# New call orders for the four compute engines ahead of the channel-pair loop, without the identity transposes

## What is computed

```python
h = rmsnorm(x, norm_mix_g)
a_val, a_gate, b_in = split(h @ w_in, [512, 1024])          # 1024 x 1536
u  = a_val * sigmoid(a_gate)
ya = silu(layernorm(causal_dwconv31(u) + conv_a_b))         # 31 taps, 512 channels
yb = (window_mean(b_in, w = 2, 4, 8, 16) - b_in) @ pool_w * pool_scale
x  = x + concat(ya, yb) @ w_out
h  = rmsnorm(x, norm_ffn_g)
gate, val = split(h @ w_up, 2)                              # 1024 x 5632
x  = x + (silu(causal_dwconv3(gate) + conv_f_b) * val) @ w_down
return rmsnorm(x, norm_final_g)
```

## Time and profile before

| | |
|---|---|
| median of 3 runs | 921.43 us (921.29 to 921.58) |
| profiled execution: its own time, first to last instruction | 918.0 us |
| TensorE busy | 897.2 us (98%) |
| VectorE busy | 690.0 us (75%) |
| GpSimd busy | 664.8 us (72%) |
| ScalarE busy | 412.6 us (45%) |
| `idle_turns` | 82 matmuls, 9.8 us busy |

### The profile page before, as it was taken

One profiled execution on the slowest core, in us unless ns is written; L12 is line 12 of the kernel. 1 busy time (PEld: TensorE's weight loads), 2 busy tenths in 40 slices (PEclk: granted clock), 3 DMA queues, 4 the chain that ended last, 5 costly groups with the idle time before them and its releaser, 6 DMA issues.

```text
span 918.0 us, 11316 instructions
## 1 busy us (share of the span) xinstructions
PE 897.2 (98%) x4088; PEld 742.8 (81%) x4088; DVE 690.0 (75%) x731; ACT 412.6 (45%) x626; POOL 664.8 (72%) x501
## 2 busy tenths in 40 slices
PE   6999999999999999999999999999999999999996
PEld 5888888888887788788888888888888888888875
DVE  6898998996787565686867768587685876858667
ACT  7566655863654422433424334243342433424335
POOL 4399998483289754977959779597795977959821
PEclk9999999999999999999999999999999999999998
DMA  8321011151001121021120211302113021121114
GB/s 286 98 73 65 1 46 47 47 161 46 0 12 35 59 79 46 12 81 46 46 92 12 84 44 46 92 12 91 35 47 92 21 83 36 46 92 29 40 47 184
DMA packets 62775, 57.74 MB, mean 63 GB/s; under 512 B 2137, under 2 KB 55897, under 8 KB 62716
## 3 DMA queue, kind: packets, MB, share of 16 engines
q1 hardware_dynamic: 62720, 57.01, 19.7%
HBM read 52.81 MB, written 4.19 MB: 62 GB/s over the span
## 4 chain that ended last, share of the span: by engine, by line
PE 82%; DVE 5%; ACT 4%; POOL 4%; issue 4%; DMA 0%; DVEq 0%; SPq 0%; POOLq 0%; ACTq 0%
PE slot L2295 81%; POOL conv L689 3%; PE slot L2331 1%; ACT prod L1072 1%; DVE act_lo L1616 1%; DVE x_sb L1938 1%; POOL tmp L675 1%; DVE tmp L1603 0%; DMA x_sb<-in_x 0%; ACT junk L959 0%; ACT act_hi L968 0%; DVE sums L1804 0%; ACT slot L1101 0%; DVE bn L1706 0%; DVE x_sb L1734 0%
## 5 line engine op out<-in xcount | busy, mean ns | idle before, releaser
L734 POOL TENSOR_TENSOR ring<-raw,ring 128x512 fp32r<-128x512 f32 x199 | 272.6, 1390 | 117.1 <-ACT ring L1148 116.9
L1148 ACT ACTIVATE ring<-raw 128x512 fp32r<-128x512 f32 x203 | 121.0, 625 | 249.1 <-POOL raw L757 117.0
L2295 PE MATMUL slot<-act_hi,ring 128*128 128x512 f32 x680 | 219.7, 390 | 1.2 <-DVE s_f L1826 0.8
L1953 DVE TENSOR_TENSOR x_sb<-x_sb,slot 128x1024 f32<-128x1024 f32 x126 | 152.6, 1217 | 55.2 <-PE slot L2295 50.1
L2295 PE MATMUL slot<-sums,ring 128*128 128x512 f32 x780 | 186.5, 389 | 0.0
L2295 PEld LDWEIGHTS slot<-sums,ring 128*128 128x128 f32 x780 | 146.4, 188 | 30.4
L2295 PEld LDWEIGHTS slot<-act_hi,ring 128*128 128x128 f32 x680 | 127.7, 188 | 28.3 <-issue 1.2
L689 POOL TENSOR_TENSOR conv<-conv,prod 128x512 f32<-128x512 f32 (+8 forms) x89 | 119.5, 1361 | 19.2 <-ACT conv L1052 10.6
L2295 PE MATMUL slot<-act_lo,ring 128*128 128x512 f32 x340 | 132.3, 389 | 0.0
L757 POOL TENSOR_TENSOR raw<-raw 128x512 f32<-128x512 f32 x88 | 120.1, 1365 | 11.5 <-POOL ring L734 3.2
L1654 DVE SCALAR_TENSOR_TENSOR slot<-x_sb,chan,slot 128x512 f32<-128x512 f32 (+18 forms) x143 | 101.7, 740 | 2.5
(11 more groups left out here) (199 smaller groups left out, 1464.4 us busy)
## 6 DMA issues: line engine op xcount, KB each, us to landing
raw<-in_w_up SPq DMA_DIRECT2D x44, 256.0 KB, 2.9
raw<-in_w_up SPq DMA_DIRECT2D x22, 512.0 KB, 3.8
raw<-in_w_down SPq DMA_DIRECT2D x22, 512.0 KB, 3.2
x_sb<-in_x SPq DMA_DIRECT2D x12, 512.0 KB, 6.1
raw<-in_w_in SPq DMA_DIRECT2D x4, 1024.0 KB, 7.2
raw<-in_w_out SPq DMA_DIRECT2D x4, 1024.0 KB, 4.9
out<-raw SPq DMA_DIRECT2D x7, 512.0 KB, 2.7
raw<-in_w_in SPq DMA_DIRECT2D x4, 512.0 KB, 9.5
```

The lines of the kernel that those rows point to most:

```text
L734: nc.gpsimd.tensor_tensor(block_at(n, 1), block_raw(n), block_at(n, 0).bitcast(F32), ALU.subtract).then_inc(block_lo, 1)
L1148: nc.scalar.activation(block_at(n, 0), block_raw(n), ACT.Copy).then_inc(block_hi, 1)
L1953: nc.vector.tensor_tensor(dst, dst, slot[part_slot(i, p)][:, :].rearrange("p (a n) -> p a n", a=2), ALU.add).then_inc(part_added, 1)
L2295: mm = nc.tensor.matmul(out_ap, st[s], mv[v], start=first and s == v == 0, stop=last and s == 1, skip_group_check=onto)
```

## The change

Only the order of calls changes, in the lists of GpSimd, ScalarE, VectorE and TensorE ahead of the loop, with the tables that count them (`PE_ORDER`, `HI_PIECES`, `LO_PIECES`, `FIRST_TAPS`, `PRODUCTS`, `ADDS`, and `LAST_TILE`). The split of the 31 taps between the engines (`LIGHT`) and the assignment of PSUM slots (`SLOTS`) stay. The two explicit waits and the four `idle_turns` on TensorE go. All other instructions are kept, each with its waits. The diff, cut to what the prediction speaks of:

```diff
 ScalarE
+            t1_hi(1)
             t1_hi(0)
-            t1_hi(1)
...
             consts_out(0)
+            product(0, 0, 2)
             half_hi(2, 0)
-            products(0, 0, 3, 5)
...
             gate_sigmoid(0)
-            product(0, 1, 1)
             first_tap(0, 1)
             product(0, 1, 2)
-            product(0, 1, 6)
-            product(0, 1, 5)
-            product(0, 1, 3)
             consts_out(1)
...
             t2_hi(1)
+            ln_std(1)
             t2_std(2)
-            ln_std(1)
             ln_z(1, 0)
...
-            for key in mixed(1)[:5]:
-                block_high(*key)
+            block_high("up", 4, B11)
+            block_high("up", 4, T1)
+            block_high("up", 4, T2)
             last_tap(3)
-            block_high(*mixed(1)[5])
+            block_high("part", 1, 0)
+            block_high("up", 4, T3)
+            block_high("up", 4, B21)
+            d3_high(1)
 VectorE
             norm_apply(IN, 5)
+            norm_apply(IN, 6)
             t1_lo(4)
-            norm_apply(IN, 6)
             norm_apply(IN, 7)
...
             make_u(0, 0)
-            taps((0, 0, 13))
+            taps((0, 0, 3))
             make_u(0, 1)
-            taps((0, 0, 5))
+            taps((0, 1, 3))
+            taps((0, 0, 8))
...
             ln_scale(0)
+            join(1, 1)
+            tap(2, 1)
+            unit_lo(7, 0)
             unit_lo(7, 1)
-            tap(2, 1)
+            diff_lo(0)
             pool_difference(2)
-            diff_lo(0)
...
-            x1(2)
-            taps((2, 1, 3))
             join(2, 1)
             join(3, 1)
-            t2_lo(1)
+            x1(2)
             ln_stat(1, 0)
             ln_stat(1, 1)
+            t2_lo(1)
...
             gate_high_half(0)
-            gate(0)
             u2_make(1)
             u3_make(1)
+            gate(0)
...
             value_high_half(3)
+            a11_low(1)
             gate_high_half(3)
             gate(3)
+            d3_low(1)
 TensorE
             t1(3)
-            pe.wait_ge(act_lo_done, LO_DONE["t1", 0])
-            idle_turns(SLOT[J_T1[0]], 0, 28)
             in_part(0, 0)
             t1(4)
+            t1(5)
             in_part(1, 0)
-            t1(5)
             t1(6)
-            idle_turns(SLOT[J_IN[0]], 1, 16)
             t1(7)
             constants()
             in_part(0, 1)
             in_part(1, 1)
             in_part(2, 0)
+            in_part(3, 0)
             in_part(2, 1)
-            in_part(3, 0)
...
             in_part(9, 0)
+            in_part(10, 0)
             in_part(9, 1)
-            in_part(10, 0)
...
             in_part(11, 1)
-            pe.wait_ge(z_done, 2)
-            idle_turns(SLOT[J_LN[0][0]], 0, 10)
             ln_back(0, 0)
             ln_back(0, 1)
-            pe.wait_ge(tokens_ready, GROUPS)
-            idle_turns(SLOT[J_POOL[0]], 0, 28)
             pool_product(0)
...
             t2(0)
+            out(2, 0)
+            out(3, 1)
             out(3, 0)
-            out(2, 3)
             t2(1)
-            out(3, 1)
-            out(3, 2)
             out(3, 3)
             ln_tokens(1, 0)
             ln_tokens(1, 1)
+            out(3, 2)
...
             product(0, T3)
             product(0, T1)
+            product(0, T2)
             product(1, T1)
-            product(0, T2)
-            product(1, T2)
             product(0, T4)
             product(1, T3)
+            product(1, T2)
             product(0, B22)
             product(1, T4)
...
```

More of the change, by code:

```diff
@@ new lines, in _ @@
+            add(1, 1, 3)
+            adds(1, 0, 8, 11)
+            add(1, 1, 4)
+            add(2, 0, 1)
+            add(1, 1, 5)
+            adds(2, 0, 2, 8)
+            add(1, 1, 6)
+            adds(2, 0, 8, 10)
+            adds(3, 0, 1, 3)
+            add(2, 0, 10)
+            add(2, 1, 1)
+            add(1, 1, 7)
+            add(3, 0, 3)
+            window(3, 0)
+            add(1, 1, 8)
+            window(3, 1)
+            adds(3, 0, 4, 6)
+            window(3, 2)
+            adds(3, 0, 6, 8)
@@ L839, in _ @@
             add(2, 1, 13)
+            adds(3, 1, 12, 14)
             s3_complete(4)
             s4_begin(4)
+            s3_complete(5)
+            factor(0, T1)
+            s4_begin(5)
             s4_complete(4)
-            factor(0, T1)
+            s4_complete(5)
+            low("up", 0, T1)
             s4_low(4)
-            s3_complete(5)
-            low("up", 0, T1)
-            s4_begin(5)
             factor(0, T2)
-            s4_complete(5)
             factor(0, T3)
@@ L877, in _ @@
             factor(2, T2)
+            low("up", 2, T2)
             factor(2, T3)
-            low("up", 2, T2)
             low("up", 2, T3)
@@ L1333, in _ @@
             first_tap(2, 0)
-            product(2, 1, 1)
-            product(1, 0, 8)
-            product(1, 1, 6)
-            products(2, 0, 2, 4)
-            product(1, 0, 9)
-            product(2, 0, 4)
+            half_hi(5, 1)
+            products(1, 1, 5, 7)
+            products(2, 0, 3, 5)
+            product(2, 0, 6)
+            gate_sigmoid(3)
+            product(2, 0, 9)
+            first_tap(3, 0)
+            half_hi(6, 0)
+            product(3, 0, 1)
+            product(2, 0, 10)
@@ L1426, in _ @@
             ln_z(1, 3)
+            t2_std(3)
             ln_silu(1, 0)
@@ L1988, in _ @@
             tap(0, 0)
+            tap(0, 1)
+            taps((0, 0, 6))
             unit_lo(3, 0)
-            tap(0, 0)
+            make_u(1)
+            tap(0, 1)
+            taps((0, 0, 3))
             unit_lo(3, 1)
-            tap(0, 0)
+            join(0, 0)
+            taps((1, 0, 2))
             tap(0, 1)
-            join(0, 0)
+            taps((1, 0, 3))
             unit_lo(4, 0)
-            make_u(1)
-            taps((1, 0, 4))
-            unit_lo(4, 1)
-            tap(1, 0)
+            tap(0, 1)
+            taps((1, 0, 7))
             tap(0, 1)
             taps((1, 0, 2))
-            taps((0, 1, 3))
             join(0, 1)
+            tap(1, 1)
             tap(1, 0)
@@ L2034, in _ @@
             unit_lo(5, 1)
+            taps((3, 0, 3))
+            unit_lo(6, 0)
+            tap(3, 0)
+            tap(1, 1)
+            taps((3, 0, 6))
+            taps((1, 1, 3))
             taps((3, 0, 2))
             tap(1, 1)
-            taps((3, 0, 5))
+            taps((3, 0, 2))
             tap(1, 1)
             tap(3, 0)
-            unit_lo(6, 0)
-            taps((1, 1, 2), (3, 0, 2))
+            tap(1, 1)
             taps((3, 0, 4))
-            join(1, 1)
             unit_lo(6, 1)
-            taps((3, 0, 3))
-            unit_lo(7, 0)
             tap(3, 0)
             join(3, 0)
+            tap(1, 1)
+            pool_difference(3)
             tap(3, 1)
-            tap(2, 1)
-            pool_difference(3)
             ln_stat(0, 0)
@@ L2079, in _ @@
             tap(3, 1)
-            unit_lo(9, 1)
-            yb_lo(3)
             tap(2, 1)
             tap(3, 1)
-            taps((2, 1, 3))
-            x1(0)
-            taps((3, 1, 3))
             tap(2, 1)
-            taps((3, 1, 2))
-            x1(1)
-            tap(2, 1)
-            norm_apply(FFN, 0)
-            taps((2, 1, 2))
-            norm_apply(FFN, 1)
-            tap(3, 1)
-            tap(2, 1)
-            t2_lo(0)
+            unit_lo(9, 0)
+            yb_lo(3)
+            unit_lo(9, 1)
             taps((2, 1, 2))
@@ L2673, in _ @@
             product(2, T2)
+            product(1, B22)
             product(2, T3)
```

510 lines of the change are left out of this document (255 added, 255 removed), and 55 rows, old and new, of tables (ADDS, HI_PIECES, LO_PIECES, PRODUCTS).

## The result

The changed kernel takes 936.50 us (median of four executions, 936.19 to 938.61), the kernel before beside it 921.50: a ratio of 1.0174, interval 1.0159 to 1.0189. The prediction said 924.0 in a range of 919 to 927. The direction was right, the size was not, and the time lies outside the range. The medians differ by 15.0 us, the ratio stands for 16.0, and the profiled spans differ by 16.5: the kernel before takes either some 919.5 or some 921.2 us (experiment 7 shows the clock's part in that), its profiled execution belongs to the faster of these groups, and the four beside the changed kernel all to the slower.

What follows compares the result with a forecast made beforehand. TensorE's matmuls (860 us) were taken as the bound, VectorE's convolution as the second. Terms 2.9 + 0.3 - 0.65 = +2.55 us on the 918.0 span, plus 3.4 carried over, gave 924.0 us, range 919.0 to 927.0.

Steps and rivals of the forecast that it cites:

- VectorE as the second bound: Convolution, 37 to 217 us: VectorE waits only 10.2 of 180 us and has 0.45 us to spare at the last join.
- VectorE's waits: Convolution: 10.7 us of waiting where 6.3 stood, so 4.4 late; 1.9 of the later 3.9 us of waits saved.
- Taps, unit splits, joins and norms ... are otherwise the same: VectorE ahead of the last join: work taken as unchanged, so the join ends 0.5 us later, at 217.2.
- Fillers at 14.67 and 31.77: TensorE's filling transposes before `in_part(0, 0)` and `in_part(0, 1)`: removal and reordering there taken at 0 and a 0.35 us gain.
- The clock's rival: Clock falls in the gap at 14.9, costing about 1.8 us: above 925.8, up to 928 with further stalls; chance 0.15.
- The rule on transposes: Skill's rule that transposes do not count for the full clock; fillers then never held it, but 0.22 against 0.12 us disagrees.
- Layer norm of half 0: Around `pool_product(0)` and `out(0, 0)`: fillers from 162.31 cost nothing; gain beyond the 0.35 taken as 0, between -0.5 and 1.0.
- the 3.25 expected at 217: TensorE at the last join: asks at 214.0, starts about 217.3; loss priced at 2.9 us, +3.25 in the ledger.
- Up projection: `u2_make(1)`, `u3_make(1)` ahead of `gate(0)` remove the 0.8 us wait at 304.04: -0.65 us, bounds -2.3 and +1.
- The 3.4 us carried over from the span to the time: Profiled span of 918.0 lies 3.4 us below the runs' median, 921.43; the difference was added to the forecast.
- what would show it: Trace signs: VectorE gaps of about 9 and 1.8 us, a TensorE wait near 217, the 0.8 us L1826 wait gone.
- The wait at the loop's start: TensorE's "issue" wait of 1.4 us at the loop's start: stays, effect 0, bounds -1.4 and +1.

Runs made afterwards that it cites:

- experiment 7: Kernel before with: new orders from the up projection's last operand on, 920.37 us; `u2_make(1)`, `u3_make(1)` ahead of `gate(0)`, 920.40; four more fillers ahead of `in_part(0, 1)`, 920.95.
- experiment 3: VectorE's first convolution calls: changed kernel with 14 taps in place of 3 ahead of `make_u(0, 1)`, 936.81 us; kernel before with 3 in place of 13, 923.88 us.
- small adds: GpSimd's convolution adds cut from 512 columns to the last 32: changed kernel 928.63 us, kernel before 918.63; only those of (2, 1), (3, 1) cut: 932.91 and 919.86.

## Why the prediction was wrong, point by point

- **VectorE as the second bound: right.** The two bounds that it named are those that made the loss.
- **Its first deadline: missed.** The prediction followed VectorE to the last join and TensorE's step at 217.12. Another such deadline lies at `ln_tokens(0, 0)`: the join of (3, 0) ended at 151.34, the transposes started at 151.63. Whatever VectorE was late there was lost for good. The single edit of experiment 3 cost 4.2 us by this way, and the sum had 0 for this place.
- **VectorE's waits: right within 1 us in the sum.** At the start 8.9 and 1.8 us were expected and 10.5 and 1.7 measured. Of the 3.9 us behind 97 us, 1.9 were to go; some 2.3 went, among them the whole wait in front of the join of (3, 0). In all, VectorE waits 3.5 us longer up to the last join, where 2.5 (4.4 less 1.9) was the sum. The view names that wait "issue"; that GpSimd's adds end it, as the prediction took it, is borne out by experiment 3, where with GpSimd's old order it stayed.
- **"Taps, unit splits, joins and norms ... are otherwise the same": the step that failed most.** Their number is the same, their durations are not. Up to the last join VectorE was busy 7.3 us longer for the same work, which the sum had at nothing without a reason, and the last join ended at 227.0, where 217.2 was forecast. The rest of those 9.8 us is the late start (`make_u(0, 0)` at 38.26, 1.15 late where 0.35 early was expected) and the waits. The kernel before could have told: `w_lo` has a mean of 1.62 us there, and single ones take 1.22.
- **Fillers at 14.67 and 31.77: wrong.** Taken at 0 and -0.35; their removal costs some 4 us by itself and 1.0 to 1.3 in the changed kernel. The clock's rival had the right mechanism, for 1.8 us at one place, where two falls follow. The argument against it, that the gap is not longer than the one behind the last matmul, took 3.2 us for it; the gap that opened was 3.6.
- **The rule on transposes.** The Trainium skill (TensorE: Matmul & The Clock Gate, Part 4) says that the full clock does not engage for transposes, since they do not count as busy in the same way, and the prediction held the row of 0.22 against 0.12 us against it. The fillers at 14.67 kept the clock in twelve executions of twelve, which goes against the rule; those at 31.77, also transposes alone, in seven of twelve. No run here explains the difference.
- **Layer norm of half 0, taken as 0: 8.4 us** (1.1 + 7.3 of the ledger) less the 3.25 expected at 217. More of GpSimd's adds run, at least in part, between the join of (3, 0) and the last one (27 against 24, of 1498 ns in the mean against 1360), and `diff_lo(0)` stands behind two weight splits and a join.
- **Up projection, -0.65: +3.4 and then -0.4.** The gain of `u2`, `u3` exists as a wait that goes and is taken by the next in line. That `norm_apply(7)` was moved behind operand splits was in the diff and not in the working.
- **The 3.4 us carried over from the span to the time: mis-sized.** In the 18 experiments an execution takes 1.7 to 1.9 us longer than its own span. The prediction set the span of one execution, with a clock of 0.997, against the median of others, whose times (921.29 to 921.58) are those of the lower clock in experiment 7. That is 1.6 us, small beside the rest.
- **Of what would show it**: the gap ahead of L1681 (now L1688) near 48.7 came at 51.8, the one of 1.8 came (1.7), the L1826 wait went. "None before 150 beyond the first" is not borne out: TensorE waited 1.6 us before 35.7 and 0.9 before 38.4, where 0.4 had stood; from there to 154 there was none. The wait at the loop's start, which was to stay at 1.4 us ("issue"), is down to 0.3; the wait near 217 did not come, because the units ahead of it were themselves late.

Of the 15 to 16 us, then: 5 to 7 are GpSimd's adds beside and ahead of VectorE (the distance with small adds), some 3 the up projection's own order (ledger, and the same stall with the old orders ahead of it), about 1 the fillers. The rest, 5 to 6 us, stays open. The new orders' waits ahead of and behind the layer norm are what is left to make it, but no run shows them by themselves: every mixture of lists made stalls of its own, and in the changed kernel the one edit that took most of VectorE's first wait away (experiment 3) gained nothing.

## What to carry to other kernels

Follow a nearly saturated engine to the first place where its partner waits without slack, not to the last; lateness there was not given back in any of these kernels. An engine's work is not a sum of fixed durations: where two engines hold each other up, moving one against the other changes busy times, and a mean far above its own smallest value is the sign. Before calling a filler or a wait useless, ask what stands next in the queue behind it: taking one wait away (the sigmoid's, the norm, `u3`) only showed the next.

## What was unexpected of the hardware

A three-column VectorE instruction took 1.85 us beside a GpSimd instruction of 2.87 and ended with it. Short GpSimd instructions were held too: a copy of one column took 0.19 us at 174.07 and 1.25 at 182.65, beside a VectorE instruction of 1.21. The splits `w_lo` ended 1.08 or 1.09 us after the GpSimd instruction that they started beside, in 19 of 21 cases. The clock fell near 37 us in some executions and not in others whose instructions up to there are the same in kind, number and order, and even with no pause of TensorE over 0.14 us ahead of it.
